# A two-layer decoder trunk on one core: block products for part of the second layer's down projection, weight sums on GpSimd

## What is computed

```python
h2 = rms_norm(x, norm2_g[l]) * (1.0 + sc2) + sh2
x = x + g2 * (jnp.square(jax.nn.relu(h2 @ w_up[l])) @ w_down[l])
```

## Time and profile before

| | us |
|---|---|
| median of 3 runs (1148.4 to 1149.76) | 1149.21 |
| the profiled execution | 1148.82 |
| its span, first to last instruction | 1147.0 |
| PE busy | 1131.8 (99%) |
| DVE busy | 858.8 (75%) |
| ACT busy | 588.4 (51%) |
| POOL busy | 163.6 (14%) |

### The profile page before, as it was taken

How to read it: one execution, slowest core, us unless ns; L and a number is a source line. 1 busy time by engine, 2 the same in 40 slices (tenths; PEclk the granted TensorE clock), 3 DMA queues, 4 the chain that set the end, 5 groups by cost and what they waited for, 6 DMA issues and landing times.

```text
span 1147.0 us, 19009 instructions
## 1 busy us (share of the span) xinstructions
PE 1131.8 (99%) x6630; PEld 1007.1 (88%) x6630; DVE 858.8 (75%) x1302; ACT 588.4 (51%) x1002; POOL 163.6 (14%) x127
## 2 busy tenths in 40 slices
PE   6999999999999999999999999999999999999998
PEld 4888888998989989989988888889989989989898
DVE  7968888689787687785668688886897575675753
ACT  6655454247454464454553555434554454554545
POOL 5393010310000000000215701013000000000003
PEclk8999999999999999999999999999999999999999
DMA  9874334624354343433409433452324233232222
GB/s 367 335 275 147 110 110 149 219 75 147 129 165 129 131 152 120 152 113 101 160 6 367 146 116 134 142 212 93 129 92 130 85 105 104 91 114 88 91 74 74
DMA packets 45748, 162.85 MB, mean 142 GB/s; under 512 B 5504, under 2 KB 6656, under 8 KB 45184
## 3 DMA queue, kind: packets, MB, share of 16 engines
q1 hardware_dynamic: 45408, 162.10, 40.3%
q10 hardware_dynamic: 288, 0.08, 0.0%
HBM read 160.06 MB, written 2.10 MB: 141 GB/s over the span
## 4 chain that ended last, share of the span: by engine, by line
PE 97%; DMA 1%; DVE 1%; SPq 0%; issue 0%; POOL 0%; ACT 0%; POOLq 0%; ACTq 0%; DVEq 0%
PE ps L385 22%; PE ps L386 22%; PE ps L387 22%; PE ps L539 8%; PE ps L541 8%; PE ps L540 8%; PE ps L602 2%; PE ps L674 1%; PE ps L657 1%; DMA arena<-ada 1%; PE ps L430 1%; PE ps L431 1%; PE ps L432 1%; PE ps L421 0%; DVE arena L1327 0%; PE ps L414 0%
## 5 line engine op out<-in xcount | busy, mean ns | idle before, releaser
L1114 DVE TENSOR_TENSOR w_lo<-w_raw,w_hi 128x1024 fp32r<-128x1024 f32 (+1 forms) x190 | 225.9, 1190 | 179.0 <-ACT w_hi L758 177.4
L758 ACT CAST w_hi<-w_raw 128x1024 fp32r<-128x1024 f32 (+1 forms) x186 | 185.1, 996 | 70.9 <-PE ps L387 64.1
L385 PE MATMUL ps<-u_hi,w_hi 128*128 128x512 f32 (+1 forms) x576 | 211.3, 367 | 0.0
L386 PE MATMUL ps<-u_lo,w_hi 128*128 128x512 f32 (+1 forms) x576 | 210.8, 366 | 0.0
L387 PE MATMUL ps<-u_hi,w_lo 128*128 128x512 f32 (+1 forms) x576 | 210.5, 365 | 0.0
L385 PE MATMUL ps<-h_hi,w_hi 128*128 128x512 f32 (+1 forms) x528 | 193.8, 367 | 0.0
L386 PE MATMUL ps<-h_lo,w_hi 128*128 128x512 f32 (+1 forms) x528 | 192.1, 364 | 0.0
L387 PE MATMUL ps<-h_hi,w_lo 128*128 128x512 f32 (+1 forms) x528 | 192.0, 364 | 0.0
L1277 DVE SCALAR_TENSOR_TENSOR x<-ps,mod,x 128x512 f32<-128x512 f32 (+1 forms) x168 | 105.2, 667 | 28.8 <-PE ps L387 28.8
L387 PEld LDWEIGHTS ps<-u_hi,w_lo 128*128 128x128 f32 x576 | 108.6, 189 | 17.6
L385 PEld LDWEIGHTS ps<-u_hi,w_hi 128*128 128x128 f32 x576 | 108.7, 189 | 16.9
(11 more groups left out here) (215 smaller groups left out, 2293.5 us busy)
## 6 DMA issues: line engine op xcount, KB each, us to landing
w_raw<-weights SPq DMA_DIRECT2D x200, 512.0 KB, 3.4
ada_raw<-ada SPq DMA_DIRECT2D x80, 512.0 KB, 4.6
arena<-ada SPq DMA_DIRECT2D x16, 512.0 KB, 15.3
x<-xT SPq DMA_DIRECT2D x2, 1024.0 KB, 6.4
tab<-tables SPq DMA_DIRECT2D x2, 1024.0 KB, 12.4
outT<-x SPq DMA_DIRECT2D x2, 512.0 KB, 3.1
out_rows<-tok_rows SPq DMA_DIRECT2D x4, 256.0 KB, 2.5
tab<-tables SPq DMA_DIRECT2D x1, 512.0 KB, 15.4
```

What stands on the lines that cost most here:

```text
L385: nc.tensor.matmul(out, wh, hi, start=first, stop=False, skip_group_check=True)
L386: nc.tensor.matmul(out, wh, lo, start=False, stop=False, skip_group_check=True)
L758: nc.scalar.copy(w_hi[:, j, cols], w_raw[:, j, cols]).then_inc(w_hi_done, 1)
L1114: nc.vector.tensor_tensor(w_lo[:, j, cols], w_raw[:, j, cols], w_hi[:, j, cols].bitcast(F32), ALU.subtract).then_inc(w_lo_done, 1)
```

## The change

1. **Block products for down.** In the second layer, in every second step of the three rounds (q = 2 and 4 of DVE's and ACT's streams, the second and fourth of PE's; six in all), `down` becomes `down_pair`: seven block products for eight, 84 matmuls of 256 columns in place of 48 of 512. An output block is two down tiles (accumulated one after the other in the halves of one bank) by half of the tokens. The host rearranges the weights of slots 2 and 3 for it.
2. **Its sums.** The four sums of the weight blocks (S1 to S4 again, in the same `s_hi` and `s_lo`) and the four sums of the u blocks (here V1 to V4: `vt_raw`, `vt_hi`, `vt_split`; 128 by 2 by 256) are made by POOL. ACT makes their hi parts, DVE their lo parts. ACT makes three more copies (`down_copied`), of 512 columns. DVE folds D7 into both token halves of tiles 6 and 7 and adds the other parts in halves.
3. **S sums on POOL.** In both layers POOL makes the S sums of `pair` too (`next_sums` in the first layer, `in_turn` in the second). In the second layer S4 is written over the first half of slot 1 (slot 3 for the down sums), so that SP may load slot 0 and 1 again only when DVE has made S4's lo part (`s_split` in `load_weight`), and slots 2 and 3 after `ds_split`.
4. **Order.** In the second layer ACT and DVE run `both_step`. Even steps take the down sums, odd steps (`plain`) the V parts. The hi part of S4 of the next pair, of u's two tiles and of slot 2 of an even step are made in ACT's stream in the next odd step.
5. **Norms.** `spread` multiplies `rstd`, broadcast along the free axis, with the identity, 128 columns at a time; the diagonal is gone from DVE and ACT.

```diff
...
+            def load_weight(l, step, j, free=True, also=None):
                 u = l * UNITS + step * SLOTS + (SLOTS + j)
+                if also is not None:
+                    sp.wait_ge(*also)
+                    if j:
+                        sp.sem_inc(down_raw_free, 1)
...
+                also = [None] * SLOTS
+                if summed is not None:
+                    also[0] = (s_split if l == DEPTH - 1 else s_raw), summed
+                if down is not None:
+                    also[2] = ds_split, down
                 for j in range(SLOTS):
-                    load_weight(l, step, j)
...
-            def spread(n, half, at):
-                pe.wait_ge(norm_r, n * 4 + half * 2)
-                nc.tensor.matmul(ps[:, RMS, at], ones[:], ssum[:, at], start=True, stop=True).then_inc(rinv_ps, 1)
+            def spread(n, half, tiles=2):
+                pe.wait_ge(norm_r, n * 2 + half)
+                for t in range(half * 2, half * 2 + tiles):
+                    mm = nc.tensor.matmul(ps[:, RMS, t * P:(t + 1) * P], rstd[:, t:t + 1].to_broadcast([P, P]), ident[:],
+                                          start=True, stop=True, skip_group_check=True)
+                mm.then_inc(rinv_ps, 1)
...
+            def down_pair(u, u_split, evac, group, i, c):
...
+                pe.wait_ge(xs_lo, u_split)
+                pe.wait_ge(evac_dve, evac)
+                pe.wait_ge(w_lo_done, u + (2 + SLOTS + 1))
+                raw(D11, 2, 0, B11, first=True).then_inc(down_ps, 1)
+                pe.wait_ge(vt_split, i * 8 + 4 * c)
+                summed(1)
+                mixed(D7, s_hi[:, S3, :], s_lo[:, S3, :], T3, first=True).then_inc(down_ps, 1)
+                summed(2)
+                copied(1)
+                mixed(D12, s_hi[:, S2, :], s_lo[:, S2, :], T2).then_inc(down_ps, 1)
+                raw(D11, 2, 1, B21).then_inc(down_ps, 1)
+                summed(3)
+                copied(2)
+                mixed(D12, s_hi[:, S1, :], s_lo[:, S1, :], T1).then_inc(down_ps, 1)
+                pe.wait_ge(w_lo_done, u + (3 + SLOTS + 1))
+                mixed(D21, w_hi[:, 3, T:2 * T], w_lo[:, 3, T:2 * T], T4).then_inc(down_ps, 1)
+                summed(4)
+                copied(3)
+                product(D12, s_hi[:, S4, :], s_lo[:, S4, :], *block(B22)).then_inc(pe_unit, 2)
             pe.sem_inc(pe_unit, SLOTS)
...
+                        if l == DEPTH - 1 and q % 2:
+                            down_pair(u, u_split, evac, 1 - q // 2, i, q // 2 + 1)
+                        else:
+                            down(u, u_split, evac, 1 - q // 2)
...
+                def both_step(i, q):
...
+                    def vt_high():
+                        act.wait_ge(mod_added, l * 24 + 24)
+                        for t in (T3, T1, T2, T4):
+                            act.wait_ge(vt_raw, i * 8 + (4 * c + 4))
+                            nc.scalar.copy(vt_hi[:, t, :, :], vt_full(t)).then_inc(vt_hi_done, 1)
...
+                    before_high(0)
+                    pair_has(1)
+                    nc.scalar.copy(ps[:, C12, HALVES[0]], ps[:, C11, HALVES[0]]).then_inc(pair_copied, 1)
+                    before_high(1)
+                    pair_has(2)
+                    nc.scalar.copy(buf_a[:, 1, HALVES[0]], ps[:, M7, HALVES[0]]).then_inc(pair_copied, 1)
+                    if plain:
+                        sum_high(p, S4)
+                    pair_has(3)
+                    nc.scalar.copy(ps[:, C21, HALVES[0]], ps[:, C12, HALVES[0]]).then_inc(pair_copied, 1)
+                    if plain:
+                        split_hi(l, step, 2)
+                    if not plain and q:
+                        down_sum_high(S3)
+                    pair_has(4)
+                    nc.scalar.activation(buf_a[:, 0, HALVES[0]], ps[:, C11, HALVES[0]], ACT.Relu).then_inc(evac_act, 1)
+                    if not plain and q:
+                        down_sum_high(S2)
+                    pair_has(5)
+                    nc.scalar.copy(buf_a[:, 1, HALVES[1]], ps[:, C12, HALVES[0]]).then_inc(pair_copied, 1)
+                    if not plain and q:
+                        down_sum_high(S1)
+                    split_hi(l, step, 3, slice(T, D) if not plain and q else slice(0, D))
+                    if plain or not q:
+                        next_high(S3, S2, S1)
+                    pair_done()
+                    nc.scalar.activation(buf_a[:, 0, HALVES[1]], ps[:, C12, HALVES[0]], ACT.Relu).then_inc(evac_act, 1)
+                    def row_relu():
+                        act.wait_ge(c2_added, l * (2 * PAIRS) + i * 8 + (2 * q + 6))
+                        nc.scalar.activation(buf_a[:, 1, :], buf_a[:, 1, :], ACT.Relu).then_inc(evac_act, 1)
+                    next_cols = slice(T, D) if q < 4 else slice(0, D)
+                    if plain or not q:
+                        split_hi(l, step + 1, 0)
+                        if plain:
+                            act.wait_ge(vt_raw, i * 8 + (4 * c + 4))
+                        u_square(tile, i * 8, evac + 2)
+                        row_relu()
+                        split_hi(l, step + 1, 1, next_cols)
+                        u_square(tile + 1, i * 8, evac + 3)
+                        if plain:
+                            u_high(tile, i * 8, tile % 8)
+                            next_high(S4)
+                            u_high(tile + 1, i * 8, tile % 8 + 1)
+                            vt_high()
+                            split_hi(l, step + 1, 2)
+                    else:
+                        down_sum_high(S4)
+                        down_has(1)
+                        act.wait_ge(mod_added, l * 24 + 24)
+                        nc.scalar.copy(ps[:, D12, :], ps[:, D11, :]).then_inc(down_copied, 1)
+                        u_square(tile, i * 8, evac + 2)
+                        row_relu()
+                        down_has(3)
+                        nc.scalar.copy(ps[:, D21, :], ps[:, D12, :]).then_inc(down_copied, 1)
+                        split_hi(l, step + 1, 0)
+                        next_high(S3)
+                        down_has(5)
+                        nc.scalar.copy(u4, ps[:, D12, :]).then_inc(down_copied, 1)
+                        u_square(tile + 1, i * 8, evac + 3)
+                        next_high(S2)
+                        next_high(S1)
+                        split_hi(l, step + 1, 1, next_cols)
...
+                    def down_rest():
+                        down_has(6)
+                        for m in range(2):
+                            stepped(m + 1)
+                            gated(6 + m, ps[:, D21, HALVES[m]], HALVES[0], down_step)
+                        dve.wait_ge(down_copied, i * 6 + 3 * c)
+                        for m in range(2):
+                            gated(6 + m, u4[:, HALVES[m]], HALVES[1], down_step)
+                        pe_has(l, i * 16 + (U_PAIR + 4 * q - 1))
+                        for m in range(2):
+                            gated(4 + m, ps[:, D12, HALVES[m]], HALVES[1], evac_dve)
...
+                    if plain:
+                        split_lo(l, step, 3)
+                        adds()
+                        next_low(S3, S2, S1)
+                        split_lo(l, step + 1, 0)
+                        split_lo(l, step + 1, 1, next_cols)
+                        u_low(tile, i * 8, tile % 8)
+                        next_low(S4)
+                        u_low(tile + 1, i * 8, tile % 8 + 1)
+                        vt_lows()
+                        split_lo(l, step + 1, 2)
+                        return
+                    residuals(i * 16 + (U_PAIR - 8 + 4 * q), 0)
+                    if q:
+                        for at in (S3, S2, S1):
+                            down_sum_low(at)
+                        split_lo(l, step, 3, slice(T, D))
+                        adds()
+                        down_sum_low(S4)
+                        down_both()
+                        split_lo(l, step + 1, 0)
+                        down_first()
+                        next_low(S3, S2, S1)
+                        split_lo(l, step + 1, 1, next_cols)
+                        down_rest()
+                    else:
+                        split_lo(l, step, 3)
+                        gate_pair(15, M_GATE2 + 6)
+                        adds()
+                        next_low(S3, S2, S1)
+                        split_lo(l, step + 1, 0)
+                        split_lo(l, step + 1, 1, next_cols)
+                        dve.wait_ge(mod_added, l * 24 + 24)
+                        residuals(U_PAIR - 4, 1)
+                    u_low(tile, i * 8, tile % 8)
+                    u_low(tile + 1, i * 8, tile % 8 + 1)
+                    next_low(S4)
+                    split_lo(l, step + 1, 2)
...
+                def in_turn(j, done, count, s3_free, s2_free, s1_free):
+                    a11, a12 = w_raw[:, j, 0:T], w_raw[:, j, T:2 * T]
```

(46 more changed lines are left out.)

305 lines of the change are left out of this document (229 added, 76 removed).

## The result

| | before | after |
|---|---|---|
| median (5 runs each), us | 1149.08 | 1190.0 (1186.63 to 1191.94) |
| ratio | | 1.0351, 95% interval [1.034, 1.0362] |
| span of the profiled execution, us | 1147.0 | 1190.1 |
| PE busy, us | 1131.8 (99%) | 1142.2 (96%) |
| DVE, ACT, POOL busy | 75%, 51%, 14% | 76%, 52%, 33% |

The account below looks back on a forecast made before the run. PE, busy 99%, was taken as the bound. Block downs -4.9, waits in two-step rounds +20.2 and last step +4.0 gave +19.3: 1168.1 us profiled, 1168.5 median; overall range 1144 to 1181, its own 1159 to 1178.

Parts of the forecast that it names:

- six block downs: Second layer's block downs on PE: 10.08 us each, 0.82 less than a plain one; -4.9 us if PE never waits.
- inside odd pairs (S parts): PE waits 1.3 us at an odd pair's seventh product for DVE's S4 lo part, five times.
- slot 0 ahead of even pairs: PE waits 0.5 us before an even pair for slot 0, after late loads and POOL sums, five times.
- copy, in even pairs: PE waits 2.2 us in an even pair for ACT's first copy, C11 to C12, five times.
- last step: After the sixth block down, the last step's first product waits for all u parts: +4.0 us.
- S sums, spread: First layer's S sums on POOL and the norms' spread without diagonal: both taken as 0.
- the lock: DVE instructions with two SBUF inputs and POOL's sums exclude each other; up to 1.24 us of DVE's time per sum.
- O: End of a block down and start of the next odd step, the zero point for the forecast's times.
- the queues absorb it: Rival: streams interleave, S4's part and the copy come in time, no PE wait; 1144.3 us, chance 0.20.
- DVE is the bound: Rival: all POOL sums fall on DVE's wanted time, two steps cost 47.9 us; 1181.9 us, chance 0.12.
- That is 4.0 us for two steps ... It needs a block down ahead, so it counts five times: Second layer's rounds: three PE waits (1.33, 0.52, 2.2) per two steps, five times, +20.2 us.
- D: Start of a block down on PE, the zero point for forecast times within it; it ends 10.08 us later.

Follow-up runs that it names:

- e0: Changed kernel without block downs: all downs plain, POOL still makes the S sums, norm spread without diagonal; 1149.07 us, ratio 1.0001.
- e9: e6 with DVE's lo part of slot 2 moved between its second and third V part in even steps; 1146.53 us, ratio 0.998.
- e2: Changed kernel, but POOL starts the V sums only after DVE has made S4's lo part; 1177.62 us, ratio 1.0242.
- e4: Changed kernel with the V sums made by DVE behind the odd step's additions, not by POOL; 1171.3 us, ratio 1.02.
- e3: Changed kernel with V casts and slot 2's cast (and DVE's parts) moved behind the even pair's second copy; 1168.49 us, ratio 1.0174.
- e5: Changed kernel with the edits of e4 and e3 together; 1154.46 us, ratio 1.0051.
- e1: Changed kernel where, in layer 2, a pair's third product waits for two S lo parts and the fifth for the third; 1191.03 us, ratio 1.0371.
- e11: Changed kernel where S1's cast in an odd step waits for three POOL sums instead of four; 1185.19 us, ratio 1.0312.
- e10: e4 where S1's cast in an odd step waits for three POOL sums instead of four; 1166.23 us, ratio 1.0141.
- e8: Kernel before, with ACT repeating the first copy of each even pair of the second layer's rounds nine times; 1173.4 us, ratio 1.0213.
- e6: e5 with even steps' u parts made before the last S parts, S1's cast waiting for three sums; 1148.54 us, ratio 0.9998.
- e7: Kernel before, with ACT repeating the first copy of each even pair of the second layer's rounds five times; 1156.33 us, ratio 1.0063.

## Why the prediction was wrong in size

| term | forecast | measured |
|---|---|---|
| six block downs | -4.9 | -4.9 |
| inside odd pairs (S parts) | 5 x 1.3 = 6.6 | 5 x 1.23 at the third product, 2 x 0.54 at the seventh: 7.2 |
| slot 0 ahead of even pairs | 5 x 0.5 = 2.6 | 0.6 to 2.6 each, seven times: 11.2 |
| copy, in even pairs | 5 x 2.2 = 11.0 | 6 waits of 1.3 to 2.8: 13.8 |
| last step | 4.0 | 4.4 |
| in no wait, half clock the largest part | none | 11.4 |
| S sums, spread | 0 | 0 (e0) |
| sum | 19.3 | 43.1 (span) |

**Right.** The mechanism, its places and its order: the lock, block downs of 10.08 us, which bring a gain only if PE never waits (e9), and S4's lo part at O + 9.9: it ends at 1018.72, O + 9.92, and O + 9.9 to 10.5 in all five such steps. That POOL's V sums start the chain is shown by e2 and e4: without them beside DVE no odd pair waits. That a long ACT tail makes the copy late is shown by e3. The last step's 4.0 (4.4) and what was put at nothing (e0) held. The rival "the queues absorb it" falls; "DVE is the bound" gave 47.9 for two steps, and 46.8 to 49.6 were measured, but for another reason: DVE stands idle for 6.39 us in that round, waiting for POOL, and e5, which gives DVE four more sums every two steps, is 35.5 us faster than the changed kernel. It is a chain that is too long, not an engine that is full.

The Trainium skill, "Perfetto Trace Analysis", section "Optimizing Scalar/DVE Operations", says that moving work between DVE and GpSimd might not help, since they share a read port. Both answers are here: the S sums moved to POOL cost nothing where PE has no DVE wait near (e0), and the V sums are better on DVE (e4: two or three of the four 0.68 each, the others 1.66 to 1.78, in its idle time) than on POOL in its rush.

**The step that failed** is "That is 4.0 us for two steps ... It needs a block down ahead, so it counts five times". It gave 5 x 4.0; in its place stand 32.2 us of gaps and, behind them, the half clock. The mechanism was right; what failed is the size of this term, and slot 0's wait above all: 11.2 where 2.6 stood. By its parts:

- *A wait left out.* I followed S4's part to the seventh product, and not the third product, which waits for three lo parts; S1's, now the third, ended 1.23 late. At the seventh PE then waits only 0.54, in two of five steps. That the third's 1.23 is about the 1.3 forecast for the seventh is chance, though e1 finds 1.3 there in three steps and 1.9 in two. (The forecast's own terms, D + 19.95, give 1.23 and not 1.33.) The wait at the third product costs almost nothing by itself (e1), as it stands in place of S4's wait, but it was there to be read in the code.
- *Slot 0: O + 22.8 forecast, O + 23.6 here and O + 25.0 two steps earlier (O = 960.63).* POOL's S1 sum starts at O + 15.2 and there at O + 16.6, for 14.7: the landing was mis-sized by 0.5 to 1.9 us, and slot 0 with it. Most of the 0.3 left is the idle time at S1's cast (see ACT's tail; e11 gains 0.2 there). Two of the seven slot 0 waits (0.6 and 1.2) come before any block down, which the forecast had ruled out. I took 4.3, from transfers of before, and two in flight. Now slots 2 and 3 come free right behind, so that four transfers run together:

```profile
w_raw<-weights SPq DMA_DIRECT2D x4, 512.0 KB, 5.4
```

(DMA issues from 965 to 985, median us to landing; from 1010 to 1030 it is 5.0.) That four in flight are the cause is argued from this row and was not tried apart.
- *ACT's tail: copy at O + 27.9 forecast, 29.3 here.* S1's cast waits for the S4 sum. I had put S2 and S1 back to back; measured 0.75 idle between. e10 and e11 show it: without this idle time each gap is 2.0 to 2.2, the forecast's 2.2, and each kernel gains 5 us.
- *Five times* was six: the first even pair waits for the copy too, though no block down is ahead of it. V casts and slot 2 already stand in ACT's tail there.
- *The clock.* No term had it. The rows of before have no wait of more than a few tenths in an MLP half, and I priced a wait of w at w. e8 shows that one of 2.8 can cost 4.3. In the changed kernel that is some 5.6 us by the estimate above.

These agree with e3. Its edit gains 21.5 us (22.9 between the profiled executions): 13.8 of copy gaps, 2.1 of slot 0's and 2.7 of the S parts' gaps. The 4.3 left are about the time outside waits that its even pairs lose less; one of them still has the half clock, behind a slot 0 gap of 2.5.

**Open.** What decides whether a wait of 2.0 to 2.8 us is followed by half the clock: equal waits had both outcomes. Why the slots that the S sums need land sooner or later (5.3 to 6.7 us behind S4's lo part). And what makes two or three matmuls of every even pair start 0.1 late in e6 and e9, 0.2 to 0.3 us a pair.

## To carry to other kernels

Where one engine is at 99% and a change loads the others, follow each raw buffer once round (freed, loaded, summed, cast, subtracted, used) and check every wait of the chain against what it really needs: here moving work behind the one copy that PE wants, the V sums to the engine that idles, the u parts forward (e6) and slot 2 forward (e9) turned +41 us into -2.3. A wait of the busy matmul engine can cost more than its length: here none of 1.2 and 2.0 us did (e7, e10), most of 2.2 did (e10, e11), and of 2.8 all in e8 and none of four in e4. A wait that disappears may reappear one product later, so read the sum of waits, not the one removed.

## Not expected of the hardware

A gap of 1.20 us in a dense stream of matmuls costs 1.27 with all that follows; a gap of 2.76 costs 4.0 to 4.3, since the granted clock is at half for about 3 us, at once or 1.3 to 1.5 us behind its end (e7, e8, six places each). At gaps of 2.0 to 2.8 in other kernels it sometimes stayed at 1.00 (e4: 2.80 of gap, pair 13.03, against 14.37 in e8). And where the half clock falls ahead of a copy that comes late anyway, it costs nothing: 13.02 and 13.03 us for a pair with and without it, in the changed kernel.
